# Splitting the per-head squares of a projection into two rounded parts, so that one-pass matmuls sum them instead of fp32 ones

## The reference, cut to what matters

```
def rms_norm(x, g):
    xf = x.astype(jnp.float32)
    y = xf * lax.rsqrt(jnp.mean(xf * xf, axis=-1, keepdims=True) + NORM_EPS)
    return (y * g.astype(jnp.float32)).astype(x.dtype)

def hybrid_mixer(h, w_in, ...):
    z = h @ w_in
    (fq, fk, fv, ff, dq, dk, dv, iq, ik, iw, ga, gb) = jnp.split(z, split_points, axis=-1)
    fq = rms_norm(fq.reshape(B, S, FOX_HEADS, HEAD_DIM), fox_qk_g[0])
    fk = rms_norm(fk.reshape(B, S, FOX_HEADS, HEAD_DIM), fox_qk_g[1])
    dq = partial_rope(rms_norm(dq.reshape(B, S, DSA_HEADS, HEAD_DIM), dsa_qk_g[0]), ...)
    dk = partial_rope(rms_norm(dk, dsa_qk_g[1]), cos_a, sin_a)
    ...
```

## Time and profile before

| | |
|---|---|
| Median of 3 runs | 1881.28 us (1880.99 to 1883.54) |
| The profiled execution's own time | 1881.4 us |
| Its span in the trace | 1879.6 us |
| TensorE matmul busy | 1869.0 us (99% of the span) |
| TensorE weight load busy | 1513.7 us (81%) |
| VectorE busy | 1070.7 us (57%) |
| ScalarE busy | 745.5 us (40%) |
| DMA | mean 111 GB/s |

### The profile page before, as it was taken

How to read it: one execution, slowest core, us unless ns; L and a number is a source line. 1 busy time by engine, 2 the same in 40 slices (tenths; PEclk the granted TensorE clock), 3 DMA queues, 4 the chain that set the end, 5 groups by cost and what they waited for, 6 DMA issues and landing times.

```text
span 1879.6 us, 24958 instructions
## 1 busy us (share of the span) xinstructions
PE 1869.0 (99%) x8930; PEld 1513.7 (81%) x8932; DVE 1070.7 (57%) x1765; ACT 745.5 (40%) x1257; POOL 57.9 (3%) x96
## 2 busy tenths in 40 slices
PE   9999999999999999999999999999999999999999
PEld 7777778888888888888888888867777888888887
DVE  6677556757766666733334356867785673333322
ACT  5455445433233233432233234447655352323221
POOL 0001000001111000000000010000000000000000
PEclk9999999999999999999999999999999999999999
DMA  5221223447777563233232332211112333332332
GB/s 185 80 64 59 68 68 112 132 138 225 229 220 227 188 206 109 92 96 100 91 99 90 123 90 90 77 57 48 56 47 77 92 99 94 99 99 92 99 110 91
DMA packets 57662, 207.70 MB, mean 111 GB/s; under 512 B 6464, under 2 KB 6592, under 8 KB 57584
## 3 DMA queue, kind: packets, MB, share of 16 engines
q1 hardware_dynamic: 46800, 167.67, 28.5%
q0 software_dynamic: 10784, 38.97, 6.6%
HBM read 204.48 MB, written 2.10 MB: 110 GB/s over the span
## 4 chain that ended last, share of the span: by engine, by line
PE 95%; DVE 2%; ACT 1%; issue 1%; DMA 0%; SPq 0%; ACTq 0%; DVEq 0%
PE PS L461 27%; PE PS L463 27%; PE PS L462 27%; PE PS L934 3%; PE PS L967 2%; PE PS L954 1%; PE PS L591 1%; PE PS L592 1%; PE PS L595 1%; PE PS L665 1%; PE PS L633 1%; PE PS L498 1%; PE PS L502 0%; PE PS L499 0%; PE PS L716 0%
## 5 line engine op out<-in xcount | busy, mean ns | idle before, releaser
L1617 DVE TENSOR_TENSOR LO<-RAW,HI 128x1024 fp32r<-128x1024 f32 x310 | 379.4, 1224 | 408.5 <-ACT HI L1133 406.7
L461 PE MATMUL PS<-XH,HI 128*128 128x512 f32 x1432 | 566.6, 396 | 1.2 <-ACT IQ L1287 0.9
L463 PE MATMUL PS<-XH,LO 128*128 128x512 f32 x1432 | 558.5, 390 | 0.0
L462 PE MATMUL PS<-XL,HI 128*128 128x512 f32 x1432 | 557.9, 390 | 0.0
L1133 ACT ACTIVATE HI<-RAW 128x1024 fp32r<-128x1024 f32 x310 | 327.6, 1058 | 524.1 <-PE PS L463 507.9
L461 PEld LDWEIGHTS PS<-XH,HI 128*128 128x128 f32 x1432 | 269.0, 188 | 60.2 <-issue 5.9
L463 PEld LDWEIGHTS PS<-XH,LO 128*128 128x128 f32 x1432 | 268.8, 188 | 56.6
L462 PEld LDWEIGHTS PS<-XL,HI 128*128 128x128 f32 x1432 | 269.2, 188 | 53.4
L463 PE MATMUL PS<-HIDH,LO 128*128 128x512 f32 x528 | 205.5, 389 | 0.0
L462 PE MATMUL PS<-HIDL,HI 128*128 128x512 f32 x528 | 205.5, 389 | 0.0
L461 PE MATMUL PS<-HIDH,HI 128*128 128x512 f32 x528 | 205.5, 389 | 0.0
(11 more groups left out here) (398 smaller groups left out, 2138.3 us busy)
## 6 DMA issues: line engine op xcount, KB each, us to landing
RAW<-weights SPq DMA_DIRECT2D x311, 512.0 KB, 3.5
ADA<-ada POOLq DMA_DIRECT2D x72, 512.0 KB, 4.7
X<-x_in SPq DMA_DIRECT2D x4, 512.0 KB, 6.8
y_out<-X SPq DMA_DIRECT2D x8, 256.0 KB, 4.5
COND<-condition POOLq DMA_DIRECT2D x1, 512.0 KB, 4.4
SQC<-squares SPq DMA_DIRECT2D x1, 320.0 KB, 9.7
TAB_P<-positions POOLq DMA_DIRECT2D x1, 256.0 KB, 5.0
POS<-positions POOLq DMA_DIRECT2D x1, 256.0 KB, 3.3
```

Source lines behind the costliest of these rows:

```text
L461: mm(bank, a, moving[0][:, t, :], start=start, stop=False)
L462: mm(bank, a, moving[1][:, t, :], start=False, stop=False)
L463: ins = mm(bank, z, moving[0][:, t, :], start=False, stop=stop)
L1617: V.tensor_tensor(LO[n0 % 3][:], RAW[n0 % 3][:], HI[n0 % 3][:].bitcast(F32), ALU.subtract)\
```

## The change

The square of each normalised tile is now split as the weights are. ScalarE copies `SQ` to a rounded `SQH`, VectorE subtracts to get the rest, `SQL`, and `head_sums` sums both parts with one-pass matmuls that accumulate, against `HALF`, a rounded copy of the two columns. TensorE waits for `SQL` instead of `SQ`. VectorE subtracts for tile j-1 in its step j, behind `split_lo` and ahead of the wait for the root of tile j-2.

```
+        SQH = at("SQH", 92, [P, 2, S], F32R)
+        SQL = [at(f"SQL{r}", A0 + (78, 63)[r], [P, S], F32R) for r in range(2)]
+        HALF = at("HALF", 206.78125, [P, 2], F32R)
 ...
 def head_sums(k):
-                    pe.wait_ge(sem("hsq"), q + 1)
+                    pe.wait_ge(sem("hsq_lo"), q + 1)
 ...
                     for b in range(NB):
                         c = 8 * (q % 2) + 2 * b
-                        ins = mm(PS[:, 3, c:c + 2], SQ[:, q % 2, b * P:(b + 1) * P], SQV["halves"][:, 0:P:64],
-                                 start=True, stop=True)
+                        tok = slice(b * P, (b + 1) * P)
+                        mm(PS[:, 3, c:c + 2], SQH[:, q % 2, tok], HALF[:], start=True, stop=False)
+                        ins = mm(PS[:, 3, c:c + 2], SQL[q % 2][:, tok], HALF[:], start=False, stop=True)
 ...   # ScalarE, project_in2, step j
                         A(SQ[:, q % 2, :], PS[:, j % 3, :], ACT.Square).then_inc(sem("hsq"), 1)
+                        act.wait_ge(sem("hsq"), q + 1)
+                        A(SQH[:, q % 2, :], SQ[:, q % 2, :], ACT.Copy).then_inc(sem("hsq_hi"), 1)
 ...   # VectorE, lambdas
+                link(V.tensor_copy(HALF[:], SQV["halves"][:, 0:P:64]))
 ...   # VectorE, project_in2, step j
                     if j > 2:
                         split_lo(FIRST["in2"] + j)
+                    if j - 1 in NRM2:
+                        q = NRM2.index(j - 1)
+                        v.wait_ge(sem("hsq_hi"), q + 1)
+                        V.tensor_tensor(SQL[q % 2][:], SQ[:, q % 2, :], SQH[:, q % 2, :].bitcast(F32),
+                                        ALU.subtract).then_inc(sem("hsq_lo"), 1)
                     if j - 2 in NRM2:
```

## The result

| | before | after |
|---|---|---|
| Median (range, 15 runs each) | 1882.62 us (1880.99 to 1889.42) | 1888.33 us (1884.86 to 1894.48) |
| Profiled execution: time, span | 1881.4, 1879.6 us | 1888.33, 1886.6 us |

The ratio is 1.0031, with a 95% interval of 1.002 to 1.0041. The change costs about 5.8 us, where the prediction said 1.9.

A forecast was written before the change was run, and what follows sets the result against it. TensorE, busy 99% of the span, was taken as the bound. Stalls of 1.16 + 0.7 + 0.1 and pairs of 0 made 1.96, rounded to +1.9 us: median 1883.2 us, likeliest 1882.1 to 1884.4, 8 in 10 1878.2 to 1885.2.

The forecast's parts named there:

- the price of a pair: Head sums: each load with its matmul stays at 0.10 us, paced by the load; term 0, ends -0.3 and +1.0 us.
- passes count after all: Rival, 15 in 100: matmul passes pace the head-sum groups, so one-pass pairs gain 4.8 us, net -2.9: 1878.4 us.
- covered stalls: Rival, 12 in 100: VectorE does its step 4 sooner or the waits are absorbed; time stays 1881.3 us.
- the first stall: TensorE's first head sums (tile 3) wait for VectorE's subtraction, late in its step 4: 1.16 us.
- The walk: Step-by-step tracing of VectorE, ScalarE and TensorE delays through the projection; puts what follows step 8's split_lo 2.4 us later.
- second stall: Transposes of step 10 wait for the late root copy of tile 7: 0.6 to 0.8 us, taken as 0.7.
- later ones: Steps 10 to 13: VectorE's root copies come later, the one of step 13 holding TensorE up by 0.1 us.
- VectorE does not recover: Rival, 12 in 100: between steps 9 and 13 each spread is late, +3.1 to +4.7 us: 1884.4 to 1886.0.
- duration follows the columns: Weight loads: duration goes by column count, 0.84 ns a column, so one-pass 128-column loads pace like fp32.
- upper bounds of the terms: Extra time at most: stalls together 2.9 us, pairs +1.0 us.
- the rule by columns: Skill's rule for weight loads: columns over 1.2 per ns, 107 ns for 128; a group 0.85 us before and after.

The follow-up runs named there:

- The repairs: Changed kernel with two PSUM banks for the spread, later GpSimd copies, or the subtraction behind the head norm: lowest 1884.62, 1886.99, 1883.40 us; together 1884.37.
- Slack given to VectorE: Changed kernel without VectorE's rotations of tile 3 and of tiles 4 to 7: median 1884.23 us, lowest 1882.67, ratio 1.0009.
- a better order alone: Changed kernel with the subtraction behind the head norm from tile 4 on, tile 3's a step sooner: median 1885.14 us, lowest 1883.40, ratio 1.0011.
- fp32 sums: Changed kernel with head sums by the old fp32 matmuls on SQ, still waiting for SQL: median 1886.91 us, lowest 1884.89, ratio 1.0021.
- work-only kernel: Kernel before plus ScalarE's copy and VectorE's subtraction, results unused, fp32 sums waiting for the square alone: median 1885.78 us, lowest 1883.58, ratio 1.0016.
- all three repairs: Changed kernel with two banks, later GpSimd copies and the subtraction behind the head norm together: median 1887.68 us, lowest 1884.37, ratio 1.0018.

## Why the prediction was right or wrong

The forecast gave a loss of over 0.2% 9 in 100, and the median lies above its range for 8 in 10 (1878.2 to 1885.2).

**Right: the bound and the price of a pair.** The argument that the loads pace the group was taken from the row with share 1.00, and holds in every kernel: 0.81 us in after, 0.81 with fp32 in its place, 0.36 with half the loads. The rival that passes count after all is dead, and so is that of covered stalls.

**Right: the first stall.** 1.16 us predicted, 1.08 measured, at the instruction named. The subtraction (0.67 to 0.69 us where it stands alone) and ScalarE's copy (632 ns) are as the nearest rows gave them. The walk holds further than that: `split_lo` of step 9 comes 1180.89 - 1.55 - 1176.98 = 2.36 us later, where it had 2.4.

**Wrong: the term "second stall", 0.7 us; it measured 1.77.** I took the root copy's end as the release. That is one of two: the transposes also wait until the head norm of the tile before has read bank 4. Before, this head norm ends 0.62 us ahead of the transposes; it stands behind the root copy on VectorE, so it comes 0.65 us later than the copy. Another 0.4 us is the subtraction, 1.09 us beside the GpSimd copies instead of the 0.69 of the row. 0.7 + 0.65 + 0.4 is 1.75, near the 1.77. Both could be read in before: the head norm's row stands behind the root copy's, and `split_lo` of that step takes 1.52 us and the root copy 0.61, instead of 1.23 and 0.43, and I kept these two without asking what the next instruction would pay.

**Wrong: the term "later ones", 0.1 us; it measured 0.87.** The same missed release. I compared the root copy's end with the transposes and found it just in time, which it is (1213.13, against 1213.94 for unhindered transposes), but 1.5 us of head norm stand behind it.

**Wrong: the rival's chance.** "VectorE does not recover" got 12 in 100 and a price of at most 4.7 us in all. Its condition is what happened: VectorE's cycle takes 7.10 and 7.92 us in steps 11 and 12 (`split_lo` to `split_lo`, 6.78 and 7.31 before), where TensorE's takes 6.84. Its course is not: the subtraction costs 0.6 us but for step 9, and there are two late waits, at steps 10 and 14, not one at each spread. That the 3.9 us between the lowest times fall in its 3.1 to 4.7 is partly luck. From the reciprocal of step 8 to the end of step 13 (1169.67 to 1206.89) VectorE was busy for 34.66 of 37.22 us already before, so 2.56 us are free, and five subtractions take 3.0 us or more. My walk through the steps took each wait by itself. The repairs show what it left out: of what was saved at step 10, a part came back at step 14. Slack given to VectorE removed both late waits, which shows where the cause lies; that it is the total of its work, and not the chain through one or two steps, is argued more than shown, since a better order alone saves 1.5 us.

**Wrong, without effect: duration follows the columns.** The prediction took 0.84 ns a column from loads of 128 and of 64 columns. The kernel before has loads of 128 columns that last as long as those of 64, those of the transposes:
```profile
L654 PEld LDWEIGHTS PS<-SQC,RB 128*128 128x128 f32 x52 | 6.4, 139 | 1.7
...
L673 PEld LDWEIGHTS PS<-SQC,VW 72*128 72x128 f32 x4 | 0.4, 140 | 0.1
```

They also follow one another faster, every 88 ns in `spread` ((1180.88 - 1180.53) / 4) and every 55 ns in the value transposes. So neither the slope nor the rule by columns that the prediction cites holds for all loads of 128 columns here. That a one-pass load paces like an fp32 one was right all the same, by the groups measured.

**A slip in the sum.** The upper bounds of the terms, 2.9 and 1.0, lead to 1885.2 and not to 1884.4. Nothing else hangs on it.

**Not in the sum: the clock.** In the profiled execution, and in that with fp32 sums, it falls some 2 us behind the wait of step 10; after 1.65 us of wait in the work-only kernel, it did not. This is the 1.7 us between 3.7 and 5.4. Falls ahead of the stage are in the median too: the stage starts 1.55 us late in after by the one near 111 us, and 6.35 late in fp32 sums, which has the long one near 755 us besides. Six of after's 15 runs lie over 8 us above its lowest, and two of before's. Whether the long waits make such falls more frequent, and so carry the median from +3.9 to +5.8, was not settled. The medians lie 3.5 us above the lowest time in after and 3.3 in the kernel with all three repairs, against 1.6 to 2.3 in before; but in the two kernels with the same wait at step 10 (fp32 sums, work only) it is 2.0 and 2.2. That speaks for neither.

## What to carry over

Matmuls with two moving columns cost their loads here: splitting the loaded operand in two took as many loads as fp32 did (0.81 us a group for both), and only fewer loads (0.36) or a narrower type (0.12) gained. When work is added to an engine with much idle time on the page, add up its busy time over the stretch in which it follows the critical engine step by step; here 57% on the page was 93% in that stretch. List every wait of the instruction that would be released, buffers that come free among them, and what the engine works beside.

## What the runs showed of the hardware

- VectorE is slower beside GpSimd's work on SBUF: 0.68 us became 0.98 to 1.65 for two-input instructions, 1.23 became 1.52 for `split_lo`. The Trainium skill has the reason (GPSIMD Engine Reference, "1. Specifications"): the SBUF interfaces are shared, with contention when a VectorE instruction has two SBUF inputs or is in a 2-port perf mode. The trace agrees for two inputs. It shows the slowing for the one-input root copy too (0.43 to 0.61 us); in which mode that copy runs, no trace here tells. When the GpSimd copies were moved, the slowing moved with them: 1.09 back to 0.68 us at step 9, and 0.98 to 1.13 us for the rotation in their new place.
- In the head sums a bf16 load of 128 columns followed the one before after 30 ns, a one-pass or fp32 one after 90 to 110. In fp32 transposes it was 88 and 55 ns, at 139 and 140 ns a load.
- The granted clock can fall to 0.50 in a single execution with TensorE busy nearly throughout; near 111 us it followed an idle time of 0.36 us which before has too (0.35) without a fall. These two falls cost 1.55 and 1.7 us. Near 755 us, in two of the 14 traces, it stayed low for some 10 us.
